# Norm scratch in the transposed slot, q and k transposed on PE in attention's last pass, and a scheduler that orders by due times, in a hybrid decoder block

## What is computed

```python
h = rms_norm(x, norm1_w)
proj = h @ w_in          # q, k, v, z, beta, decay of mixer A; q, k, v of mixer B; two gates
# mixer A: causal conv of width 4 + SiLU on q, k, v, then the gated delta rule, 8 heads x 128,
#   per-head RMSNorm times SiLU(z), y_a = o_a @ w_proj_a
# mixer B: rotary on the first 32 of 128 dims, dilated windows (128,1), (512,4), (2048,16),
#   4 heads each; the three groups are joined by their softmax denominators, y_b = o_b @ w_proj_b
merged = sigmoid(ga) * y_a + sigmoid(gb) * y_b
x = x + merged @ w_out
h2 = rms_norm(x, norm2_w)
x = x + (silu(gate) * up) @ w_down        # gate, up = h2 @ w_gate_up
return rms_norm(x, final_norm_w)
```

## Time and profile before

| | us |
|---|---|
| three runs | 3902.23, 3715.72, 3337.03 |
| median of the three | 3715.72 |
| the profiled execution | 3335.06 |
| its span on the slowest core (core 3) | 3333.2 |
| spans of the 8 cores | 3312.4 to 3333.2 |
| PE busy | 3154.6 (95% of the span) |
| DVE busy | 1800.0 (54%) |
| ACT busy | 1588.6 (48%) |
| POOL busy | 922.4 (28%) |

### The profile page before, as it was taken

One profiled execution on the slowest core, in us unless ns is written; L12 is line 12 of the kernel. 1 busy time (PEld: TensorE's weight loads), 2 busy tenths in 40 slices (PEclk: granted clock), 3 DMA queues, 4 the chain that ended last, 5 costly groups with the idle time before them and its releaser, 6 DMA issues.

```text
span 3333.2 us, 63345 instructions; the slowest of 8 cores (3312.4 to 3333.2 us)
## 1 busy us (share of the span) xinstructions
PE 3154.6 (95%) x25108; PEld 2006.4 (60%) x25108; DVE 1800.0 (54%) x4140; ACT 1588.6 (48%) x4177; POOL 922.4 (28%) x1253
## 2 busy tenths in 40 slices
PE   5899999999999999999984899999999999999998
PEld 3578888788777776777773444444444444444443
DVE  5766676667877787777732565565211212212212
ACT  4756666666666766777752333333211312212212
POOL 4433443434544444444321111211211000000000
PEclk9999999999999999999997999999999999999999
DMA  8332452422442236221339343343475254445422
GB/s 165 105 71 63 77 84 66 74 58 61 66 77 50 53 59 82 51 55 51 60 94 183 114 152 121 112 133 118 92 129 96 89 83 84 106 64 114 89 45 82
DMA packets 347609, 293.85 MB, mean 88 GB/s; under 512 B 178608, under 2 KB 310320, under 8 KB 347312
## 3 DMA queue, kind: packets, MB, share of 16 engines
q1 hardware_dynamic: 225264, 210.44, 23.2%
q0 software_dynamic: 122048, 79.37, 17.9%
HBM read 276.23 MB, written 67.70 MB: 103 GB/s over the span
## 4 chain that ended last, share of the span: by engine, by line
PE 87%; DMA 5%; DVE 3%; ACT 2%; POOL 1%; issue 1%; SPq 0%; DVEq 0%; POOLq 0%; ACTq 0%
PE psf L394 84%; PE psf L397 3%; DMA arena<-arena 2%; ACT arena L400 1%; DVE arena L431 1%; DVE arena L422 1%; POOL arena L422 1%; ACT arena L405 1%; DMA arena<-gcT_d 1%; DMA arena<-c_maskq 1%; DMA ob_d<-arena 0%; DMA arena<-w_down 0%; DMA oaT_d<-arena 0%; DMA arena<-dn_norm_w 0%; DVE arena L454 0%
## 5 line engine op out<-in xcount | busy, mean ns | idle before, releaser
L394 PE MATMUL psf<-arena 128*128 128x512 bf16 (+3 forms) x22050 | 3076.4, 296 | 105.9 <-ACT arena L400 44.1
L394 PEld LDWEIGHTS psf<-arena 128*128 128x128 bf16 x22050 | 1842.6, 103 | 1183.1 <-ACT arena L400 52.2
L422 DVE TENSOR_TENSOR arena<-psf,arena 128x128 f32<-128x128 f32 (+3 forms) x944 | 471.8, 523 | 835.4 <-PE psf L394 679.5
L422 POOL TENSOR_TENSOR arena<-arena 128x512 f32<-128x512 f32 (+4 forms) x704 | 648.5, 932 | 942.9 <-DVE arena L431 417.4
L400 ACT ACTIVATE arena<-psf 128x512 f32<-128x512 f32 (+2 forms) x770 | 421.1, 569 | 878.4 <-PE psf L394 751.7
L405 ACT CAST arena<-psf 128x512 bf16<-128x512 f32 (+1 forms) x896 | 471.5, 547 | 297.5 <-PE psf L394 291.9
L431 DVE SCALAR_TENSOR_TENSOR arena<-arena,psf 128x512 bf16<-128x512 f32 (+2 forms) x640 | 339.6, 546 | 196.4 <-PE psf L394 149.7
L400 ACT ACTIVATE arena<-arena 128x512 f32<-128x512 f32 (+6 forms) x592 | 273.2, 485 | 312.5 <-DVE arena L422 170.2
L422 DVE TENSOR_TENSOR arena<-arena,psf 128x512 bf16<-128x512 bf16 (+1 forms) x640 | 328.5, 523 | 142.2 <-PE psf L394 138.0
L397 PE MATMUL psf<-ident_b,arena 128*128 128x128 bf16 x2348 | 263.1, 223 | 52.4 <-DVE arena L431 36.1
L405 ACT COPY arena<-psf 128x256 f32<-128x256 f32 (+2 forms) x467 | 226.6, 491 | 173.7 <-PE psf L397 127.0
(11 more groups left out here) (34 smaller groups left out, 708.3 us busy)
## 6 DMA issues: line engine op xcount, KB each, us to landing
arena<-w_gate_up POOLq DMA_DIRECT2D x40, 1024.0 KB, 12.9
arena<-x SPq DMA_DIRECT2D x64, 512.0 KB, 4.4
ob_d<-arena SPq DMA_DIRECT2D x192, 130.0 KB, 2.0
arena<-ob_d SPq DMA_DIRECT2D x32, 780.0 KB, 5.0
arena<-gcT_d SPq DMA_DIRECT2D x64, 256.0 KB, 3.5
x_d<-arena SPq DMA_DIRECT2D x32, 512.0 KB, 2.9
arena<-x_d SPq DMA_DIRECT2D x32, 512.0 KB, 4.0
out<-arena SPq DMA_DIRECT2D x32, 512.0 KB, 2.7
```

The costliest lines, as they stand in the source:

```text
L394: P.emit("pe", lambda e: e.matmul(out, lhsT=lhsT, rhs=rhs, start=start, stop=stop), reads=reads, excl=excl, cost=c)
L422: P.emit(eng, lambda e: e.tensor_tensor(out=out, in0=in0, in1=in1, op=op), reads=reads, writes=writes, excl=excl, cost=c)
```

## The change

There are four edits. (1) The thrown-away squares of the first norm are written into the tile's own slot of `hT`, so the squaring no longer waits for the transposes that read `xn[z]`. (2) From J = 160 on, the four tiles of q and k are transposed by PE into bank 5 and copied out by DVE, in place of the DMA transpose. (3) `prio` is no longer the longest path. Each instruction belongs to a lane with a start and an end, and its due time is spread evenly over its place in the lane; the earliest due time goes first. (4) The guessed cost of a plain transfer falls from 4.0 + bytes / 80e3 to 3.0 + bytes / 150e3 (bytes counted at 4 per element), which for a 512 KB attention weight load is 17.1 before and 10.0 now. A shift of the attention buffers by 144 words goes with it.

```diff
+MIX_END = 1600.0
@@ emit
+        ins.prio = 0.0
+        self.lane[2].append(ins)
@@
+    def use_lane(self, name, t0=0.0, t1=0.0):
+        if name not in self.lanes:
+            self.lanes[name] = (t0, t1, [])
+        self.lane = self.lanes[name]
@@ schedule
+        for t0, t1, li in self.lanes.values():
+            for n_, i in enumerate(li):
+                i.prio = -(t0 + (t1 - t0) * n_ / len(li))
@@
-            for i in reversed(L):
-                m = 0.0
-                for s_ in i.succ:
-                    if s_.prio > m:
-                        m = s_.prio
-                i.prio = m + i.cost + LAT
@@ DMA
-    ... dma=True, cost=4.0 + nb / 80e3)
+    ... dma=True, cost=3.0 + nb / 150e3)
@@ build_program
+        P.use_lane("norm", 0.0, 75.0)
@@ phase1, tile
-        ACTV(P, xn[z], xt[s], AF.Square, reads=[xk], writes=[nk, "p1ss%d" % i], accum_out=k.stat2[:, i:i + 1])
+        ACTV(P, hT[:, :, i * 128:(i + 1) * 128], xt[s].rearrange("p (a b) -> p a b", a=8), AF.Square, reads=[xk], writes=["hT%d" % i, "p1ss%d" % i], accum_out=k.stat2[:, i:i + 1])
@@ phase2a
+        P.use_lane("stream%d" % sid, 22.0 + 12.0 * sid, MIX_END)
@@ phase2b, proj
-        DMAT(P, qkT[:, sl, :, :], tm, reads=[tk + "r", tk + "s"], writes=["t_qkT%d" % sl, tk])
+        if J >= 5 * NT:
+            pt = psf[5][:, :].bitcast(BF16)
+            for x in range(4):
+                TRN(P, pt[:, x * 128:(x + 1) * 128], tm[:, x, :], k.ident_b[:], reads=[tk + "r", tk + "s", "ident_b"], excl=["psf5"])
+            CPY(P, "dve", f2(qkT[:, sl, :, :]), pt[:, 0:512], reads=[tk], writes=["t_qkT%d" % sl], excl=["psf5"])
+        else:
+            DMAT(P, qkT[:, sl, :, :], tm, reads=[tk + "r", tk + "s"], writes=["t_qkT%d" % sl, tk])
@@ phase2b, the loop over J
+    P.use_lane("att", 80.0, MIX_END)
+        if J == 5 * NT:
+            P.use_lane("last", MIX_END, MIX_END + 120.0)
@@ phase3a, phase3b
+    P.use_lane("out", MIX_END + 120.0, MIX_END + 640.0)
+    P.use_lane("ffn", MIX_END + 640.0, MIX_END + 1580.0)
```

More of the change, by code:

```diff
@@ L53, in __init__ @@
         self.heirs = []
+        self.lanes = {}
+        self.lane = None
     def emit(self, eng, fn, reads=(), writes=(), excl=(), dma=False, cost=0.5):
@@ L438, in DMA @@
     nb = 4 * 128 * _fsz(out if len(out.shape) >= len(in_.shape) else in_)
-    P.emit(eng, lambda e: e.dma_start(out=out, in_=in_), reads=reads, writes=writes, dma=True, cost=4.0 + nb / 80e3)
+    P.emit(eng, lambda e: e.dma_start(out=out, in_=in_), reads=reads, writes=writes, dma=True, cost=3.0 + nb / 150e3)
 def ASEL(P, out, in_, op, fill, nb, w, reads=(), writes=()):
@@ L923, in phase2b @@
     assert A.off <= k.off_att - 144, (A.off, k.off_att)
-    A.off = k.off_att
+    A.off = k.off_att - 144
     P.heir("tn_", P.keys("p1nw"))
```

## The result

The changed kernel took 3352.06 us (median of nine runs, 3337.90 to 3851.60) beside 3340.51 us (3335.62 to 3902.23) of the kernel before in the same job. The ratio is 1.0044 with a 95% interval of 1.0023 to 1.0065. Some executions of either kernel show a lower granted clock on the cores of one die or of both and take up to 17% longer; every ratio and average in this document leaves those out. The forecast was 3319 us, 0.5% less; its range holds the result, but it forecast a gain and there was a loss.

What follows compares the result with a forecast made beforehand. PE was taken as the bound, busy 1419.0 of 1440 us in the mixed stage, with 123.6 us idle around it to aim at. From 3335.06 us, -25 + 22 - 13 = -16 gave 3319 us; range 3262 to 3398.

Steps and rivals of the forecast that it cites:

- The streams in step: Mixed stage: both recurrence streams run at nearly the same place, so weight loads and chains coincide; 5 us more.
- The last pass: Last attention pass, from 1640 us: PE transposes replace DMA transposes and the order moves; -13 us, bounds -60 and +28.
- Start, -25: First 200 us: small loads first, scratch edit, norm by due time, mask and clock; -25 us, bounds 0 and -40.
- the mask's wait: Start of attention: PE's 7.42 us wait for the mask's load shrinks but doesn't vanish; -4 us.
- Mixed stage, +22: 200 to 1640 us: early-planned weight loads (17) and coinciding streams (5) cost 22 us; bounds 0 and +50.
- early weight loads: Mixed stage: attention weight loads planned 7 us too soon stall PE at 5 pass changes; half of 35 us, 17.
- The bound of 50: Mixed stage's upper bound: the worst window's 5.7 us lost at each of 8 pass and head changes, +50.
- The rival of the fixed queue: Mixed stage: PE's fixed queue stands for DVE, ACT and transfers; idle 21 to 107 us, 3383 us; chance 0.13.
- Its cadence: Last pass: a unit takes 5.9 us under the weight loads, 4.3 once they have landed, instead of 7.4.
- the POOL block: Last pass: POOL issues 17 weight loads in one block, 17 x 0.93 = 16 us, with hardly a unit meanwhile.
- -54 + 47 + 8: Last pass, forecast -54 + 33 + 8: units gone before the loads, longer stretch behind (158 for 125), streams ending together.
- the rival that stores take their place: Last pass: stores replace transposes as the wait, a unit stays at 7.4 us; 3328 us, chance 0.14.

Runs made afterwards that it cites:

- e7: The changed kernel with the two recurrence streams' due times 24 us apart at both ends; ratio 0.9918 to the kernel before.
- e11: The kernel with streams 24 us apart, but with DMA transposes in the last attention pass; ratio 0.9964 to the kernel before.
- e1: The kernel before with only the last pass's PE transposes of q and k, still longest path and old DMA costs; time fell by 0.54%.
- e2: The kernel before with due times alone (old DMA costs, old scratch, DMA transposes); 16 us won at the start, 33 lost in the mixed stage, 12 in the last pass.
- e3: The kernel before with due times and the lowered DMA cost, old scratch and DMA transposes; mixed stage lost 59 us, against 61 with the old costs.
- e15: The kernel with streams 24 us apart, but with the old DMA costs everywhere; ratio 1.0027 to the kernel before.
- e6: The kernel before with the last pass's PE transposes and the scratch edit, still longest path and old DMA costs; ratio 0.9921 to the kernel before.

## Why the prediction was wrong

Three steps failed. The streams in step, a term of 5 us, cost 22. The last pass, a gain of 13, was level. And the spread of the cores, which isn't in the sum, cost 12. With 5 us less than forecast at the start and 11 us won behind the last pass, where none was forecast, this makes +11 of the forecast -16; by the ratio it is +15.

**Start, -25: right.** 20 us won, within the bounds; the mask's wait and the third squaring's went as written, and the first squaring came at 14.5 (11 to 15 promised). The last load of x left between 121 and 127 (120 promised), and PE idled 50.5 us in the first 200, not 38. Right sum, but that is partly luck: waits for weight loads came in (10.4 us on core 3), and of the parts the norm's order brings 0 to 10 us.

**Mixed stage, +22: 31 measured, and for the other reason.** The terms were 17 for early weight loads and 5 for the streams in step. They measured 1 to 4 and 22 (59 less 37); the term that I put last was four times too small. The bound of 50 was also a little off by its own working, 8 x 5.7 = 46. PE idled 37.7 us between 200 and 1640, near the 40 promised, but mostly not at the pass changes: on core 3 the waits for w_in and for a pass's first transposes are 10.8 us of it. So the match is luck. I saw that both streams run at nearly the same place, but gave it 5 us for the whole stage, where each of 32 blocks pays some 0.7 us. The rival of the fixed queue named the place rightly, but not the lever, and it ended far under its 86.

**Last pass, -13: nothing measured (-1).** This step failed as a sum. Its cadence held: behind the loads 13 units took 56 us (attention of J = 172 ended at 1801.5, of 185 at 1857.7), 4.3 each as forecast; the loads ran 93 us (89). But under the loads a unit took 6.9 and not 5.9 (J = 166 to 172), and the POOL block was 28.6 us and not 16, since I took 17 issues at their own price and left out that with 14 semaphores the last three wait for landings. The row maximum's waits for the stores came (8 from 1700 on, 21.1 us), and the DMA transposes are 160. From the first load to the full output stage it was 172 us (1713 to 1885), not 158, inside my own bounds. With 47 for 33 my sum is -54 + 47 + 8 = +1.

**PE transposes.** "VectorE: DVE Perf Modes" of the Trainium skill, section "The three transpose paths", has 390 ns for one on TensorE. In the changed kernel four go by in 0.23 us:

```profile
1814.98 0.39 PE L404 MATMUL psf<-ident_b,arena 128*128 128x128 bf16 x4
1815.21 2.02 PE L401 MATMUL psf<-arena 128*128 128x256 bf16 x17
```

That is 57 ns each, so the trace doesn't agree with the page's figure as a price in a queue, and the row was the right guide. "Advanced Engine Details and Errata", section "X-Bar Transpose (TRN2)", has transpose DMAs as fast as ordinary ones, with which the landing times of the earlier trace rows nearly agree; it stands beside the rival that stores take their place. In the changed kernel that rival is nearly what happened, but e7 against e11 shows 13 to 18 us for the same edit (and e1 14, with more moved than the transposes). Why it is worth nothing between streams 2 to 11 us apart is open.

**Behind the last pass: not in the prediction.** 11 us were won from 1900 on. They belong to the lowered cost under due times (33 to 23 from e2 to e3, 32 to 23 from e15 to e7), 4 us under longest path. I costed the edit only where it could hurt.

**The slowest core.** Even a right sum would have missed the metric, which is the largest of eight spans. My ledger ends at -1; the slowest core still lost, as its distance from the average grew from 9 to about 21 us. Part of it is seen at the start of the feed-forward stage: w_gate_up arrives in time on the early cores and 4.5 to 7.6 us late on the others. This wait comes with the lowered DMA cost and never without it. That the cores slow each other's loads fits the landing times and wasn't tested.

## What to carry to other kernels

When an order is rewritten, look first at what now runs in step: two chains may now wait together, and a half period's offset between them was worth 1.3% here. But it depends on the rule: under longest path the same chains in step cost nothing. A planner's guessed cost moves the whole order, so its effect isn't at the operation it belongs to: the same edit cost 23 us under one rule and nothing under the other; test it by itself under the rule that it will run with. Compare the new rule with the plain edits under the old one, too: e6, longest path with the transposes and the scratch alone, ran at 0.9921, as fast as the best spread of due times that I tried with the same costs as the change (e7, 0.9918). And with eight cores the forecast is of the slowest: an edit that leaves the mean alone may still widen the spread.

## What the runs showed of the hardware

A 1 MB weight load of the same instruction landed 9.1 us after issue on core 0 and 17.5 us on core 3 in one execution, with 16 us between their issues. POOL's issues of weight loads took 0.93 us each (1.85 for two); the 6.24 and 6.77 us at the 16th and 17th of the block are the program's own doing, through its 14 semaphores. And transposes on PE went by every 57 ns in a queue of matmuls.
